# Retention scores: the two heads of a pair alternate key block by key block

## The reference, cut to what matters

```python
def retention(q, k, v, g, norm_g):
    q = rotary(q.reshape(bsz, s_len, C_HEADS, C_HEAD_DIM), pos) * (C_HEAD_DIM ** -0.5)
    k = rotary(k.reshape(bsz, s_len, C_HEADS, C_HEAD_DIM), pos)
    ...
    scores = jnp.einsum('bnthd,bnshd->bnhts', qc, kc) * d_intra
    y_intra = jnp.einsum('bnhts,bnshe->bnthe', scores, vc)
    kv = jnp.einsum('bnshd,bnshe->nbhde', kc * k_dec[:, :, None], vc)
    ...
    _, s_prev = lax.scan(step, jnp.zeros(kv.shape[1:], kv.dtype), kv)
    y_cross = jnp.einsum('bnthd,nbhde->bnthe', qc * q_dec[:, :, None], s_prev)
    y = (y_intra + y_cross).reshape(bsz, s_len, C_HEADS, C_HEAD_DIM)
    ...
    return jax.nn.silu(g) * y
```

## Time and profile before

| | us |
|---|---|
| median of three runs | 2554.78 (2554.11 to 2557.25) |
| the profiled execution | 2554.77 |
| its span in the trace | 2552.6 |
| TensorE busy | 2407.1 (94%) |
| VectorE busy | 1280.5 (50%) |
| ScalarE busy | 920.9 (36%) |
| mean granted TensorE clock | 0.981 of full |

### The profile page before, as it was taken

One profiled execution on the slowest core, in us unless ns is written; L12 is line 12 of the kernel. 1 busy time (PEld: TensorE's weight loads), 2 busy tenths in 40 slices (PEclk: granted clock), 3 DMA queues, 4 the chain that ended last, 5 costly groups with the idle time before them and its releaser, 6 DMA issues.

```text
span 2552.6 us, 28851 instructions
## 1 busy us (share of the span) xinstructions
PE 2407.1 (94%) x11244; PEld 1717.4 (67%) x11244; DVE 1280.5 (50%) x2170; ACT 920.9 (36%) x1608; POOL 162.6 (6%) x190
## 2 busy tenths in 40 slices
PE   8899996999898999699988999999999999999998
PEld 7655864444575477454446777888887768788887
DVE  4765544333458645523334445666523444666632
ACT  4575542111337745311113224444323213444421
POOL 1301002000021100200001000000000000000000
PEclk9999998999999999899998999999999999999999
DMA  4100406999520023489992212233334212233331
GB/s 176 50 1 34 155 20 255 394 394 394 193 67 17 1 83 124 158 318 394 394 358 92 75 50 83 91 99 99 99 99 133 74 50 76 82 99 99 93 108 56
DMA packets 131830, 359.74 MB, mean 141 GB/s; under 512 B 10992, under 2 KB 12016, under 8 KB 131440
## 3 DMA queue, kind: packets, MB, share of 16 engines
q1 hardware_dynamic: 131408, 357.48, 39.5%
q10 hardware_dynamic: 288, 0.42, 0.1%
HBM read 355.76 MB, written 2.10 MB: 140 GB/s over the span
## 4 chain that ended last, share of the span: by engine, by line
PE 85%; DVE 8%; ACT 4%; POOL 1%; issue 1%; DMA 0%; SPq 0%; POOLq 0%; DVEq 0%; ACTq 0%
PE ps L970 11%; PE ps L972 11%; PE ps L971 11%; PE ps L1188 9%; PE ps L984 6%; PE ps L985 6%; PE ps L986 6%; PE ps L1210 4%; PE ps L1108 3%; PE ps L1081 3%; PE ps L1089 2%; PE ps L1268 1%; PE ps L1150 1%; PE ps L1151 1%; PE ps L958 1%
## 5 line engine op out<-in xcount | busy, mean ns | idle before, releaser
L1855 DVE TENSOR_TENSOR wlo<-stage,whi 128x1024 fp32r<-128x1024 f32 x268 | 327.8, 1226 | 438.1 <-ACT whi L1330 437.6
L970 PE MATMUL ps<-hTh,whi 128*128 128x512 f32 x1232 | 489.8, 398 | 7.7 <-DVE hTl L1814 7.7
L972 PE MATMUL ps<-hTh,wlo 128*128 128x512 f32 x1232 | 480.0, 390 | 0.0
L971 PE MATMUL ps<-hTl,whi 128*128 128x512 f32 x1232 | 479.7, 389 | 0.0
L1330 ACT ACTIVATE whi<-stage 128x1024 fp32r<-128x1024 f32 x268 | 281.3, 1053 | 238.7 <-PE ps L986 238.2
L970 PEld LDWEIGHTS ps<-hTh,whi 128*128 128x128 f32 x1232 | 231.4, 188 | 61.5 <-issue 14.2
L971 PEld LDWEIGHTS ps<-hTl,whi 128*128 128x128 f32 x1232 | 231.5, 188 | 51.0 <-issue 4.3
L972 PEld LDWEIGHTS ps<-hTh,wlo 128*128 128x128 f32 x1232 | 231.3, 188 | 48.9
L1814 DVE SCALAR_TENSOR_TENSOR t<-ps,vecs,t 128x511 f32<-128x511 f32 (+1 forms) x176 | 131.6, 748 | 42.2 <-ACT t L1303 39.1
L1971 DVE TENSOR_REDUCE st<-ps 128x1 f32<-128x512 f32 (+1 forms) x160 | 100.9, 631 | 73.3 <-PE ps L1081 70.2
L984 PE MATMUL ps<-whi,inh 128*128 128x512 f32 x352 | 136.9, 389 | 0.0
(11 more groups left out here) (293 smaller groups left out, 3731.8 us busy)
## 6 DMA issues: line engine op xcount, KB each, us to landing
stage<-in_wpk SPq DMA_DIRECT2D x268, 512.0 KB, 3.6
wt<-in_wg SPq DMA_DIRECT2D x48, 512.0 KB, 11.8
stage<-in_wd SPq DMA_DIRECT2D x48, 512.0 KB, 12.4
ws<-in_wu SPq DMA_DIRECT2D x44, 512.0 KB, 11.5
ws<-in_wg SPq DMA_DIRECT2D x40, 512.0 KB, 11.4
wt<-in_wu SPq DMA_DIRECT2D x40, 512.0 KB, 11.6
wq<-in_wd SPq DMA_DIRECT2D x28, 512.0 KB, 12.5
wt<-in_wd SPq DMA_DIRECT2D x24, 512.0 KB, 12.0
```

Of the source, the lines that this page charges most:

```text
L970: pe.matmul(o, h, ah, start=k == 0, stop=False)
L971: pe.matmul(o, h, al, start=False, stop=False)
L972: t = pe.matmul(o, lo, ah, start=False, stop=k == 7)
L1855: ve.tensor_tensor(M.wlo[i % NW][:, :], M.stage[i % NSTAGE][:, :], f(M.whi[i % NW][:, :]), ALU.subtract).then_inc(*S.wlo.mark(("w", i)))
```

## The change

The score step keeps its eight matmuls per pair and their sizes. Before, a tick issued blocks 0 to 3 of head 2p, and the next one blocks 0 to 3 of head 2p+1. Now a tick issues block 0 of both heads and block 1 of both, and the next one block 2 of both and block 3 of both. The number of ticks stays, and so does the place of `rvalues`, a tick later.

```diff
-        def intra(h, then):
-            for j in range(4):
-                u = self.take()
-                self.do("intra", l, h, j, u)
-                self.drop(u)
+        def intra(p, keys, then):
+            for j in keys:
+                for h in (2 * p, 2 * p + 1):
+                    u = self.take()
+                    self.do("intra", l, h, j, u)
+                    self.drop(u)
             self.later.append(then)

         def pair(p):
-            intra(2 * p, lambda: intra(2 * p + 1, lambda: values(p)))
+            intra(p, (0, 1), lambda: intra(p, (2, 3), lambda: values(p)))
```

## The result

The changed kernel takes 2540.96 us (median of 4 runs, 2539.8 to 2543.02) against 2554.72 before: 13.8 us less, a ratio of 0.9945 with a 95% interval of 0.9928 to 0.9962. Run again beside the experiments it took 2540.86 us. The prediction said 2537.4 with a range of 2534.3 to 2543.0: the sign and the range hold, and 3.6 of its 17.4 us did not arrive. Where they went is the more useful part of this case.

The account below looks back on a forecast made before the run. The prediction took TensorE's own stream to bound the kernel. Removing 37.6 us of score groups and adding 20.2 us of paired ones saves 17.4 us, so 2554.8 becomes 2537.4 us, range 2534.3 to 2543.0.

Parts of the forecast that it names:

- The bound: In the score stretches TensorE is always busy, so a microsecond off it is one off the kernel if VectorE keeps up.
- The unknown price: Score matmuls on different row halves were priced like value matmuls on column halves: 20.2 us instead of 37.6; chance 0.82.
- The rate argument: Score outputs: two passes side by side write 2 x 512 columns in 0.43 us, the same rate as the projection's matmuls.
- VectorE: In the first tick it becomes late for its rotation by about 0.6 us, with slack about 1.6 us; cost nothing.
- Rival 1: Score groups: passes start only in stream order, so half an overlap, 12.3 us gained, 2542.5 us; chance 0.07.
- The semaphore tail: Score ticks: a skill-page price of 26.3 ns per further increment would add 1.3 us, making the sum 2538.7.
- rival 4: Shorter ticks: VectorE or weight splits become late and TensorE waits, giving back half the gain, 8.7 us; 2546.1 us; chance 0.03.
- The range: Whole kernel: 2534.3 us from bare streaming alone, up to 2543.0 us to reach over Rival 1; nearly 0.9 by its chances.

Follow-up runs that it names:

- one_tick: Changed kernel with all eight score matmuls of a pair alternating heads in one tick and none in the next; 2535.03 us, ratio 0.9931.
- same_half: Changed kernel with both heads' score matmuls reading partitions 0 to 63, the odd heads' own scores left out; 2555.22 us, ratio 1.0002.
- apart: Changed kernel with, within each tick, both blocks of one head first and then both of the other; 2540.98 us, ratio 0.9944.
- one_tick_again: Second run of the changed kernel with a pair's eight score matmuls alternating in one tick, for an ordinary trace; 2534.92 us, ratio 0.9925.
- warm: Changed kernel with identity transposes in place of the three waits at the border to the feed-forward stage; 2537.0 us, ratio 0.9928.
- best: Changed kernel with one-tick order plus identity transposes in waits at feed-forward, expert and second layer's mixer borders; 2532.53 us, ratio 0.991.
- one_tick_apart: Changed kernel with a pair's eight score matmuls in one tick, four of one head, then four of the other; 2546.92 us, ratio 0.9971.

## Why the prediction was right, and where it was off

- **The bound.** "A microsecond taken off TensorE is a microsecond off the kernel", as long as VectorE keeps up: right in the stretch (74.00 of 74.00 us busy), and wrong as a statement about the kernel. What leaves the stretch early arrives at the border early, and there the time of arrival has a price of its own.
- **The unknown price.** Taken from the column halves, 0.82 sure. Measured: the row halves cost the same, 20.5 us where 20.2 was summed. The difference is the cost of entering a group: I took 0.17 for one and 0.22 for the other, and both cost 0.21 (1.70 - 1.49 and 0.85 - 0.64). The removed 37.6 us are removed; the gain in the groups is 17.1 and not 17.4 us. What a group costs outside itself (see one_tick) is in neither sum, and cancels, since 16 groups stay 16. same_half shows that it is the halves.
- **The rate argument** for two writers of all 128 partitions held: two passes side by side take no longer than one.
- **VectorE.** Predicted late for its rotation, split through at 6.6 us of an 8.2 us tick; measured 6.4 of 8.23. Nobody waited. TensorE's busy time fell by 14.0 us (2407.1 to 2393.1) and not by the 17 that the prediction looked for, since the falls count as busy time.
- **Rival 1** (passes only in the order of the stream, 2542.5 us) stands 1.5 us from the measured median and would look confirmed by the time alone. The groups refute it: 1.70 us where it needs 2.1, and apart shows a pass overtaking three. That the time came out near its number is chance: the falls of the clock took nearly what half an overlap would have cost. The Trainium skill, "TensorE: Matmul & The Clock Gate", The mechanism, says that matmuls start and end strictly in program order; the traces here disagree, at least between fp32 passes of different halves.
- **The semaphore tail.** By the further 26.3 ns per increment of the Trainium skill, "TensorE: Matmul & The Clock Gate", The cost: per-tile semaphore tail, a tick's own cost would have been larger than the value group's by 0.08 us; it is 0.21 against 0.17. Against the groups before, which signal as often, it is 0.21 to 0.22, and in one_tick_again, with eight signals, 0.22 (2.36 - 2.13). So the traces don't agree with a cost of that size in the stream of matmuls, and the change adds none.
- **The step that was missing: rival 4.** "Given back" was there, but only with VectorE and the weights as the way, each with slack. The clock was read inside the stretches alone, where it was 1.00, and taken as a constant of the kernel. The border 60 us behind them, with three waits that sum to 2.1 us, was not looked at, though the earlier trace rows names a wait next door and the page had the clock at 0.981 over the span. A fall there costs 1.7 us, two of them 3.3 us, and that is nearly all of the 3.6 us by which the sum was off. It could not have been predicted surely from the trace of before alone, but it could have been a rival with its price, and that trace has the price: the same 25 transposes stand at 2.95 us at the borders to the feed-forward stages and at 4.62 us at 1949.08 us.
- **The range** held because it reached over rival 1, for another reason than the one given.

## What to carry to other kernels

Where a matmul uses only 64 partitions, on the input side or the output side, look for its partner on the other half and issue the two next to each other; the busy time of the line halves and the mean duration stays. Keep them within two matmuls of each other, since a pass overtook three others here and not four. And when TensorE's stream gets shorter, look at the waits behind the stretch, at the borders between stages: whether the clock survives them can change with a shift of one or two microseconds, in either direction, so a result a few microseconds off the sum may be the clock and not the change. Cheap matmuls in place of such waits took the chance out of it here: in the traces of warm and best none of the filled borders has a fall.

## What the runs showed that I had not expected

- 3.4 us of added TensorE work cost nothing in one kernel (2540.17 against 2540.86 us) and 6.9 us in the other (2562.17 against 2555.3).
- A pass of the free half overtakes three passes that stand ahead of it in the program, but not four: groups of 1.71 us (apart) and 3.96 us (one_tick_apart).
- Alternating heads was not needed in the change as made; having both heads in one tick was (apart, 2540.98 us).
- A score group costs about as much around it (0.2 us, in the gap ahead and in the rotation behind) as inside it, so one group fewer per pair brought 3.0 us and not 1.6.
- warm came out 0.4 us from the prediction's sum by chance: its trace lacks three falls, one of them at a border where nothing was filled.
